# Gates of every second group of a dense gate matrix put on by GpSimd, all groups one step behind their compare

## What is computed

```
scores = einsum('thcd,hckd->thck', qh, sub_keys); sv, si = top_k(scores, 16)
cv, ci = top_k(sums of the two halves' scores, 16)        # 8 heads x 16 experts of a token
experts = i1 * 128 + i2; gates = softmax(cv)
act = gelu(expert_u[experts] . x); out = sum(act * gates * expert_v[experts])
```

## Time and profile before

| what | value |
|---|---|
| median of 3 runs | 4089.5 us (4086.95 to 4093.19) |
| the profiled execution | 4082.31 us, its span on the core 4080.5 us |
| mean granted PE clock | 0.973 of full speed |
| busy over the span: PE, DVE, ACT, POOL | 3818.6, 2399.2, 1682.2, 739.6 us |
| dense stage: first compare to last eviction | 1127.0 to 1518.2 us |
| L3319 gates on ACT | 384 activations, 96 groups |
| L3308 and L3309 compares on DVE | 96 each |

### The profile page before, as it was taken

How to read it: one execution, slowest core, us unless ns; L and a number is a source line. 1 busy time by engine, 2 the same in 40 slices (tenths; PEclk the granted TensorE clock), 3 DMA queues, 4 the chain that set the end, 5 groups by cost and what they waited for, 6 DMA issues and landing times. The chain is left out here.

```text
span 4080.5 us, 57384 instructions
## 1 busy us (share of the span) xinstructions
PE 3818.6 (94%) x23037; PEld 3308.2 (81%) x23037; DVE 2399.2 (59%) x4212; ACT 1682.2 (41%) x2809; POOL 739.6 (18%) x582
## 2 busy tenths in 40 slices
PE   8999989989888879999999999997999999799998
PEld 5788767777787879999999999775777877677887
DVE  6455323447879767777777777556643345674333
ACT  4523332444456883333333333436532233554222
POOL 0112000253104513222233222201000010101000
PEclk9999999989999999999999999998999999899999
DMA  5211334433345459888888887321143432202332
GB/s 206 69 40 43 112 132 176 166 97 92 111 144 166 163 187 307 292 278 285 284 275 287 278 289 226 119 69 52 54 134 114 144 124 89 63 30 83 97 94 78
DMA packets 209193, 617.30 MB, mean 151 GB/s; under 512 B 18464, under 2 KB 68640, under 8 KB 205088
## 3 DMA queue, kind: packets, MB, share of 16 engines
q1 hardware_dynamic: 168352, 465.76, 35.2%
q0 software_dynamic: 40576, 147.87, 10.4%
HBM read 583.67 MB, written 29.88 MB: 150 GB/s over the span
## 5 line engine op out<-in xcount | busy, mean ns | idle before, releaser
L510 DVE TENSOR_TENSOR wlo<-raw,whi 128x1024 fp32r<-128x1024 f32 x576 | 714.7, 1241 | 704.8 <-ACT whi L502 704.2
L544 PE MATMUL ps<-hhi,whi 128*128 128x512 f32 (+1 forms) x2824 | 1075.2, 381 | 12.3 <-ACT uact L3372 8.9
L546 PE MATMUL ps<-hlo,whi 128*128 128x512 f32 (+1 forms) x2824 | 1049.2, 372 | 0.4 <-DVE hlo L2609 0.4
L502 ACT ACTIVATE whi<-raw 128x1024 fp32r<-128x1024 f32 x660 | 693.4, 1054 | 605.4 <-PE ps L555 455.6
L555 PE MATMUL ps<-hhi,wlo 128*128 128x512 f32 (+1 forms) x2824 | 663.2, 373 | 0.0
L544 PEld LDWEIGHTS ps<-hhi,whi 128*128 128x128 f32 x2824 | 533.1, 189 | 115.3 <-issue 22.7
L546 PEld LDWEIGHTS ps<-hlo,whi 128*128 128x128 f32 x2824 | 533.4, 189 | 68.9 <-issue 3.6
L555 PEld LDWEIGHTS ps<-hhi,wlo 128*128 128x128 f32 x2824 | 511.5, 188 | 72.1 <-issue 4.8
L544 PE MATMUL ps<-ag_hi,whi 128*128 128x384 f32 x1024 | 342.1, 334 | 0.0
L546 PE MATMUL ps<-ag_lo,whi 128*128 128x384 f32 x1024 | 342.0, 334 | 0.0
L510 POOL TENSOR_TENSOR wlo<-raw,whi 128x1024 fp32r<-128x1024 f32 x85 | 209.2, 2468 | 328.9 <-ACT whi L502 328.0
(11 more groups left out here) (629 smaller groups left out, 6160.2 us busy)
## 6 DMA issues: line engine op xcount, KB each, us to landing
raw<-w_in SPq DMA_DIRECT2D x151, 512.0 KB, 3.7
raw<-peer_u SPq DMA_DIRECT2D x128, 512.0 KB, 4.6
raw<-peer_v SPq DMA_DIRECT2D x128, 512.0 KB, 4.3
raw<-w_mod SPq DMA_DIRECT2D x96, 512.0 KB, 3.7
raw<-w_gate SPq DMA_DIRECT2D x66, 512.0 KB, 3.6
raw<-w_up SPq DMA_DIRECT2D x66, 512.0 KB, 3.5
raw<-w_down SPq DMA_DIRECT2D x66, 512.0 KB, 3.5
gate_dram<-stage SPq DMA_DIRECT2D x24, 1024.0 KB, 4.7
```

The costliest lines, as they stand in the source:

```text
L502: a.x.activation(whi[n % NW][:], raw[i % NRAW][:], ACT.Copy, bias=0.0, scale=1.0).then_inc(*a.gives("hi", i))
L510: e.x.tensor_tensor(wlo[n % NW][:], raw[i % NRAW][:], whi[n % NW][:].bitcast(F32), ALU.subtract).then_inc(*e.gives(*lo_sig(i)))
L544: t.x.matmul(o, w, p.hi, start=grp.opens and k == 0, stop=False)
L546: t.x.matmul(o, w, p.lo, start=False, stop=False)
```

## The change

The gates of odd groups are moved from ACT to POOL, in one product of 128x512 with the gates' columns broadcast (`along`). The gates of even groups stay on ACT as they were. All gates of group k are now put in step k + 1 and the matmuls and the eviction of group k in step k + 3, so there is one more step (NQ + 3). A helper names the semaphore that tells that a group has its gates. The conditions of the planner and the waits of PE go by that helper. Nothing else is changed in the text of the kernel; the planner makes its order anew.

```diff
--- before.py
+++ after.py
@@ -3274,17 +3274,21 @@
             e.wait_ge("split_v", "c0", x)
         e.wait_ge("route_t", "scores", 15)
 
+    def gated(k):
+
+        return ("dense_g", k) if k % 2 else ("dense_a", k, "gated")
+
     def dense_tensor(t):
         yield When("context attended")
         freed[IOTA_BANK] = [("dense_v", NQ - 1, "b")]
-        for k in range(NQ + 2):
+        for k in range(NQ + 3):
             if k < NQ:
                 yield When(("tile", GT * k // 128))
-            if k >= 2:
-                n = k - 2
-                yield coming("key", ("dense_a", n, "gated"), ("dense_v", n, "b"))
+            if k >= 3:
+                n = k - 3
+                yield coming("key", gated(n), ("dense_v", n, "b"))
                 b = take(t, "key", ("dense", n), ("dense_a", n, "out"))
-                t.wait_ge("dense_a", n, "gated")
+                t.wait_ge(*gated(n))
                 t.wait_ge("dense_v", n, "b")
                 for x in range(GT):
                     ins = t.x.matmul(four(b, x), ea[n % 4][:, x, :], eb[n % 4][:, x, :], start=True, stop=True)
@@ -3311,15 +3315,15 @@
 
     def dense_scalar(a):
         dense_free(a)
-        for k in range(NQ + 2):
-            if k < NQ:
-                a.wait_ge("dense_v", k, "a")
+        for k in range(NQ + 3):
+            if 1 <= k <= NQ and k % 2:
+                a.wait_ge("dense_v", k - 1, "a")
                 for x in range(GT):
-                    n = GT * k + x
-                    ins = a.x.activation(ea[k % 4][:, x, :], ea[k % 4][:, x, :], ACT.Copy, bias=0.0, scale=gT[:, n:n + 1])
-                ins.then_inc(*a.gives("dense_a", k, "gated"))
-            if k >= 2:
-                n = k - 2
+                    n = GT * (k - 1) + x
+                    ins = a.x.activation(ea[(k - 1) % 4][:, x, :], ea[(k - 1) % 4][:, x, :], ACT.Copy, bias=0.0, scale=gT[:, n:n + 1])
+                ins.then_inc(*a.gives(*gated(k - 1)))
+            if k >= 3:
+                n = k - 3
                 s, c = n // 4, GT * (n % 4)
                 a.wait_ge("dense_t", n)
                 if s >= 2:
@@ -3328,17 +3332,25 @@
                                bias=0.0, scale=1.0).then_inc(*a.gives("dense_a", n, "out"))
             yield
 
+    def dense_gpsimd(g):
+        for k in range(NQ + 3):
+            if 1 <= k <= NQ and k % 2 == 0:
+                e = ea[(k - 1) % 4]
+                g.wait_ge("dense_v", k - 1, "a")
+                g.x.tensor_tensor(e[:], e[:], along(gT[:, GT * (k - 1):GT * k]), ALU.mult).then_inc(*g.gives(*gated(k - 1)))
+            yield
+
     def dense_sync(y):
-        for k in range(NQ + 2):
-            if k >= 2 and (k - 2) % 4 == 3:
-                s = (k - 2) // 4
-                y.wait_ge("dense_a", k - 2, "out")
+        for k in range(NQ + 3):
+            if k >= 3 and (k - 3) % 4 == 3:
+                s = (k - 3) // 4
+                y.wait_ge("dense_a", k - 3, "out")
                 y.x.dma_start(gate_dram[s].rearrange("p j t -> p (j t)"), stage[s % 2][:].rearrange("p j t -> p (j t)")).then_inc(
                     *y.landing(f"stage{s % 2}", s))
             yield
         gates_sync(y, 0)
     streams["dense"] = {"tensor": dense_tensor, "vector": dense_vector, "scalar": dense_scalar,
-                        "sync": dense_sync}
+                        "gpsimd": dense_gpsimd, "sync": dense_sync}
```

## The result

| | median us | range | runs | ratio to before, 95% interval |
|---|---|---|---|---|
| before | 4089.61 | 4086.95 to 4093.19 | 4 | |
| the change | 4049.01 | 4047.97 to 4052.06 | 4 | 0.9897 [0.9886, 0.9908] |
| the change again, beside 9 runs of before (4091.24) | 4047.11 | 4046.77 to 4048.93 | 4 | 0.9895 [0.988, 0.9911] |

The change is faster by 40.6 us in the first measurement and by 44.1 in the second. Forecast were 12.8 us (4076.7, range 4060 to 4092): the sign was right, the size was a third of the real one, and the result lies 11 us outside the range.

A forecast was written before the change was run, and what follows sets the result against it. TensorE (PE), busy 94% of the span, was taken to bound the kernel. The terms -4.8 - 6 - 8 + 3 + 3 = -12.8 us, carried over to the median of 4089.5, gave 4076.7 us, range 4060 to 4092.

The forecast's parts named there:

- The drained part: End of the dense stage, nothing else left to run: 1.25 us a group, 53.4 us against 58.2, 4.8 less.
- rival 2: Drained part: PE, ACT and the ring take turns, 1.45 us a group, 8 us more, 4084.7; chance 0.15.
- The number of drained groups: Dense groups left to the drained part, set by the planner: 40 instead of 34.
- The 6 groups of POOL's lag: POOL's lag makes the planner push 6 groups out of the woven part, 6 us less there.
- the count matters little: Drained and woven parts: if no groups moved, the two terms would be 12.3 and 0, nearly the same sum.
- the term for the woven part: Dense steps strewn between context network and mixer: gates one step behind their compare free ACT, 8 us less.
- the bound: Woven part: the most the one-step-later order can touch, from PE's waits for ACT, 19.3 us.
- Rival 1: Woven part: ACT's waits were the trouble, all 19.3 us come back, POOL costs 2; -28, 4061.4; chance 0.18.
- POOL's price: Woven part, some 28 products: 3 us more for queued splits, 3 more for POOL and DVE in each other's way.
- The other term: Woven part: POOL's splits (wlo) queue behind its products and PE waits for them, 3 us more.
- rival 4: POOL holds the woven part up, 28 products at 1.27 us each: 36 in place of 6, 4106.5; chance 0.09.
- under a third of its time: DVE's work with two SBUF inputs, the kind POOL disturbs, put at under a third of DVE's time.

The follow-up runs named there:

- e2: The change with all gates back in the step of their compare and matmuls two steps behind; odd groups' product stays on POOL; 4073.41 us.
- e1: The change with all gates kept on ACT, one step behind their compare, and no POOL products; 4055.01 us.
- e5: The kernel before with only ACT's gates moved one step later, matmuls and evictions still two steps behind their compare; 4053.37 us.
- e11: The change in its planned order, plus 48 POOL products by ones on eb of the even groups; 4064.22 us.
- e8: The change with POOL's product only for odd groups from 64 on, the other gates on ACT; 4047.12 us.
- e10: The change in its planned order, plus a second POOL product by ones on ea ahead of each gate product; 4067.33 us.

## Why the prediction was right in sign and wrong in size

**The drained part: right.** The prediction took 1.25 us a group; it is 1.19 to 1.20, DVE's two compares as read in the earlier trace rows, and rival 2 (another beat) did not come. With the same count the sum was 2.7 us too careful.

**The number of drained groups: right for the half that was looked at, wrong as a whole.** The 6 groups of POOL's lag are e2's 42 against 36. That the later steps pull groups forward (25 with them alone) was not seen; together it is 34, two fewer than before. That the count matters little holds: 19 or 34 groups make the same time. So the wrong direction of the count, six more forecast and two fewer measured, cost the forecast only 2 us, and that is luck.

**The step that failed** is the term for the woven part: "What the one-step-later order can touch at all is 24.0 - 15.5 + 7.1 + 3.7 = 19.3 us", and the 8 us taken from it. With the count of groups left as it was, my terms for the woven part come to -8 + 3 + 3 = -2 us; like for like it was -22.3, and with the later steps alone (e1) -26.8, beyond the bound. That is 20 of the 25 us by which the stage differs from the forecast. 2.7 more are the drained part; the last 2 are a matter of counting: I had 6 groups leave the woven part, and 2 entered it.

The bound was made of the rows in which PE waits for ACT. Those rows did give about what I took from them, 10.0 us for the 8. But DVE is the busiest engine next to PE here, and what makes DVE late makes PE late in rows that name DVE, or none. DVE's largest wait was for ACT's whi, 32.2 us. It stood on record in the earlier trace rows, where I read the 26.9 us of work in the line and not the wait behind it; and ACT's 83.6 us for the compare I took for one engine's harmless waiting, where it was half of a loop, DVE to ACT to DVE. That DVE, busy for 80% of the part, would be the next to be waited for was my argument for taking little. A fifth of DVE's time, 68 us, was idle, and 32.2 of it were this wait. The runs showed in the bound's place what the loop was worth: with the gates one step later as the only edit (e5, its order planned anew) DVE's wait fell to 6.8 us and the woven part became 24.6 us shorter like for like. Rival 1 named the right place, but its price, -19.3 + 2, had the same bound in it, so the whole range stopped 11 us short.

**POOL's price: near in the net, and by luck.** The forecast was 3 + 3 us for the products in the woven part. e1 (no products) gained 26.8 us there like for like and the change 22.3: they cost 4.5 us net. They cost in DVE's time: without the compares, DVE's instructions of the woven part take 189 us in e1 and 197 in the second profile of the change (sums over the traces). The other term, splits queued behind products, is not seen (PE waits 0.3 us for wlo where it waited 1.3). Gross the price is twice the forecast: 32 added products lengthened the woven part by 12.4 us in e11, 0.39 us each, where I took 6 for 28 and rival 4 began at 0.67. One reading behind it was wrong: I put DVE's work with two SBUF inputs at under a third of its time, and by the trace before it is 133 of the 266 us that DVE is busy in the woven part. That the relief of ACT gives the rest back is argued; no run has the one without the other.

## What to carry to other kernels

Before bounding what a moved instruction can give back, follow the waits of the busiest engines beside PE too, and look for two engines that wait for each other in turn: where A waits for B and B for A in the same rounds (here 83.6 and 32.2 us in all), PE's own rows show only the end of it. A step's lag between a producer and its in-place consumer was worth nine tenths of this change by the medians. Giving work to another engine paid in the drained part (e8 against e1, 8 us), where DVE's compares, with an operand in PSUM, were not disturbed by it; the products in the woven part, beside DVE's other work, made no difference to the time that the runs can tell (the change against e8).

## What the runs showed of the hardware

I had expected only DVE instructions with two SBUF inputs to suffer from POOL. In the second profile of the change a cast of 128x256, one input, that takes 0.29 us by its median took 2.47, from 0.06 us behind the start of a POOL split to 0.15 behind its end (DVE, then POOL):

```profile
1256.12 2.47 DVE L3173 CAST sif<-siu 128x256 f32<-128x256 uint32 x1
```
```profile
1256.06 2.38 POOL L510 TENSOR_TENSOR wlo<-raw,whi 128x1024 fp32r<-128x1024 f32 x1 [0.69 <-ACT whi L502]
```

In the same execution the 12 tensor_scalar instructions at L3198 range from 0.211 to 2.446 us; the compares with their PSUM operand and the MAX8 instructions show nothing of the kind. The Trainium skill, page "SBUF — State Buffer", section "Who interferes with whom", counts copies, casts and tensor_scalar among what can take the pair of SBUF ports that DVE and GpSimd share, when they enter a two-port mode, and has the later one blocked for the earlier one's whole length; the trace agrees with both (2.47 us beside 2.38).

It goes the other way too. In the change POOL's gate product takes 1.040 us by its median over its 48, and 1.487 at most. In e10 one takes 2.97: it starts 0.93 us behind the start of a DVE instruction with two SBUF inputs and ends 0.90 behind its end, as if most of its own 1.04 us had only begun there (DVE, then POOL):

```profile
1287.61 3.00 DVE L3225 TENSOR_TENSOR eqv<-rank,cst 128x2048 f32<-128x2048 f32 x1
```
```profile
1288.54 2.97 POOL L3346 TENSOR_TENSOR ea<-ea,gT 128x512 f32<-128x512 f32 x1
```

Multiplying by a tile of ones repeated for four tokens took 1.282 by the median (e10), with a shortest of 1.266, where the gates' columns, each repeated along a row, took 1.040, with a shortest of 1.029: on POOL the pattern of the second operand mattered by a quarter here.
